# Two expert layers: the last block's results stay on chip and come back by products, row copies wait for the comparisons, parameter loads change queue

## Reference, cut to what matters

```python
x = layer_norm(ALPHA * x + h, ln_g[i, 0], ln_b[i, 0])      # 512 tokens x 1024
# moe_ffn: one of 4 groups of 4 experts for each token, the best 2 of the group
s = sigmoid(x @ w_router); biased = s + b_router
grp = argmax(sum of the two best in each group)
gate = s of the two best experts of grp, divided by their sum
f = sum over experts of ((silu(x @ w_gate) * (x @ w_up)) * gate) @ w_down
x = layer_norm(ALPHA * x + f, ln_g[i, 1], ln_b[i, 1])
```

## Time and profile before

| what | value |
| --- | --- |
| time, median of 3 runs | 2315.68 us (2313.99 to 2317.23) |
| the profiled execution | 2315.13 us, its span in the trace 2313.3 us |
| PE busy in the span | 2025.1 us, 88% |
| DVE busy | 1392.0 us, 60% |
| ACT busy | 946.2 us, 41% |
| POOL busy | 143.0 us, 6% |

### The profile page before, as it was taken

The page is one execution under the profiler, slowest core; times in us unless marked ns, Lnnn a source line. Parts: engine busy times, 40 slices in busy tenths (PEclk is TensorE's granted clock), DMA queues, the critical chain, the costliest instruction groups (busy, mean ns, idle before and its releaser), DMA issues. The chain is left out here.

```text
span 2313.3 us, 29677 instructions
## 1 busy us (share of the span) xinstructions
PE 2025.1 (88%) x11832; PEld 1715.4 (74%) x11832; DVE 1392.0 (60%) x1932; ACT 946.2 (41%) x1387; POOL 143.0 (6%) x196
## 2 busy tenths in 40 slices
PE   5999988979999898999959999299968888599993
PEld 5888878869999785876748888178956666488882
DVE  7864545435545444433379999445036665789995
ACT  4643336221000002534357777221125561477772
POOL 3441000000000000000030000000000000200000
PEclk9999999979999998999969999699879999699996
DMA  7433112232322222220249999422420002189993
GB/s 212 108 74 96 65 55 86 65 63 91 110 73 92 73 76 77 92 74 36 91 143 375 383 397 388 121 77 91 133 57 1 1 1 79 55 344 385 398 390 118
DMA packets 165944, 326.58 MB, mean 141 GB/s; under 512 B 33392, under 2 KB 101792, under 8 KB 165680
## 3 DMA queue, kind: packets, MB, share of 16 engines
q1 hardware_dynamic: 133872, 282.92, 34.6%
q0 software_dynamic: 10720, 30.34, 4.1%
q10 hardware_dynamic: 21216, 11.42, 2.0%
HBM read 299.41 MB, written 19.99 MB: 138 GB/s over the span
## 5 line engine op out<-in xcount | busy, mean ns | idle before, releaser
L2256 PE MATMUL ps<-m_ws,m_xbT 128*128 128x512 f32 x1344 | 314.5, 390 | 0.0
L2256 PEld LDWEIGHTS ps<-m_ws,m_xbT 128*128 128x128 f32 x1344 | 251.8, 188 | 52.1
L2446 DVE TENSOR_TENSOR m_ws<-ring,m_ws 128x2048 fp32r<-128x2048 f32 x112 | 256.1, 2289 | 32.5 <-ACT m_ws L2313 30.0
L1621 PE MATMUL ps<-ffT,ff_ws 128*128 128x264 f32 (+1 forms) x1056 | 241.7, 324 | 4.4 <-DVE ff_ws L431 4.4
L2313 ACT CAST m_ws<-ring 128x2048 fp32r<-128x2048 f32 x112 | 213.3, 1910 | 66.2 <-PE ps L2256 38.4
L1621 PEld LDWEIGHTS ps<-ffT,ff_ws 128*128 128x128 f32 x1056 | 176.8, 190 | 20.2 <-DVE ff_ws L431 4.5
L1621 PE MATMUL ps<-ffT_lo,ff_ws 128*128 128x264 f32 (+1 forms) x528 | 170.3, 323 | 0.0
L2289 PE MATMUL ps<-m_ws,m_hT 128*128 128x512 f32 x672 | 166.8, 397 | 0.0
L2289 PEld LDWEIGHTS ps<-m_ws,m_hT 128*128 128x128 f32 x672 | 122.1, 188 | 23.1
L2443 DVE TENSOR_TENSOR m_ws<-ring,m_ws 128x2048 fp32r<-128x2048 f32 x56 | 128.2, 2290 | 9.5 <-ACT m_ws L2311 8.7
L458 PE MATMUL ps<-fd_ws,fd_xs 128*128 128x512 f32 x528 | 121.9, 394 | 6.7 <-DVE fd_xs L431 6.7
(11 more groups left out here) (521 smaller groups left out, 4260.2 us busy)
## 6 DMA issues: line engine op xcount, KB each, us to landing
ring<-in_moe_w_gate SPq DMA_DIRECT2D x112, 512.0 KB, 5.4
ring<-in_moe_w_up SPq DMA_DIRECT2D x112, 512.0 KB, 7.4
ring<-in_moe_w_down SPq DMA_DIRECT2D x56, 1024.0 KB, 8.0
ring<-in_w_up SPq DMA_DIRECT2D x22, 1024.0 KB, 5.1
ring<-in_w_in SPq DMA_DIRECT2D x16, 1024.0 KB, 6.6
ring<-in_gla_w_in SPq DMA_DIRECT2D x12, 1024.0 KB, 5.3
ring<-in_w_down SPq DMA_DIRECT2D x11, 1024.0 KB, 4.9
ring<-in_nsa_w_in SPq DMA_DIRECT2D x10, 1024.0 KB, 6.7
```

The lines of the kernel that those rows point to most:

```text
L1621: ins = nc.tensor.matmul(ps[:, bank, 0:b - a], w[j][:, k, s * P:(s + 1) * P], x[l][:, k, a:b], start=(k == 0 and j == l), stop=(k == KD - ...
L2256: ins = nc.tensor.matmul(ps[:, it % 2, :], xbT[:, blk % 2, a, 4 * half + k, :].bitcast(F32R), v[b][:, k, :], start=(half == 0 and k == 0 a ...
L2446: ins = V.tensor_tensor(o, x.rearrange("p (j k w) -> p j k w", k=4, j=2), x0, ALU.subtract)
```

## The change

It has four parts. (1) In the head of `moe_stage`, POOL's row copies wait until all one-hots are made; two of the four roundings of ACT, and their rests on DVE, move behind the sigmoid and behind the group choice; `lo(0)` and `lo(1)` move behind the slot numbers; the table for the sigmoid is loaded earlier; blocks 2 and 3 are loaded one unit later. (2) In its tail, block 6 is not copied, stored and fetched: the gather from DRAM takes blocks 0 to 5 (block 6 of `y_slots` is zeroed once) and waits only for these; its sum with `h` comes first; the output of block 6 is split in two halves and 16 products with a transposed one-hot bring its rows to the tokens in PSUM, where `residual` adds them. One-hots of the last block are made in unit 20 and transposed in unit 23. (3) `residual` and `squares` now make LayerNorm's sums in the expert stage, and the norm stage (kind "summed") only makes the reciprocal root and normalises. (4) The parameter loads at the heads of `gla_project` and `nsa_project` are issued by POOL, and DVE waits for them after `lo(1)`.

```diff
 norm_stage:
-            st = self.sb(ctx, tag + "_st", [P, 5, 8])
+            st = self.lst if kind == "summed" else self.sb(ctx, tag + "_st", [P, 5, 8])
...
+                if kind == "summed":
+                    act.wait_ge(self.squared, TT * self.n_ln)
...
-                    for i, (r, t, c0) in enumerate(tiles):
+                    for i, (r, t, c0) in enumerate(tiles if kind != "summed" else ()):
 residual:
-        link(self.nc.vector.scalar_tensor_tensor(y, y, ALPHA, new, ALU.mult, ALU.add, accum_out=st[:, 3, t:t + 1]))
+        link(self.nc.vector.scalar_tensor_tensor(y, y, scale, new, ALU.mult, ALU.add, accum_out=st[:, 3, t:t + 1]))
 gla_project and nsa_project: scalar, vector, gpsimd
-                for to, frm in loads:
-                    act.dma_start(to, frm).then_inc(loaded, 16)
...
-                dve.wait_ge(loaded, 16 * len(loads))
                 S.lo(dve, 0)
                 S.lo(dve, 1)
+                dve.wait_ge(loaded, 16 * len(loads))
...
+                for to, frm in loads:
+                    pool.dma_start(to, frm).then_inc(loaded, 16)
 moe_stage, tensor:
+                        if it == EG * LAST - 1:
+                            pe.wait_ge(hot, 2 * TT)
+                            pe.wait_ge(xt_lo, 2 * (LAST - 2) + 2)
+                            for t in range(TT):
+                                ins = nc.tensor.transpose(ps[:, 7, P * t:P * (t + 1)], hot_flat[:, P * t:P * (t + 1)], self.ident[:])
...
+                pe.wait_ge(yl_out, 2)
+                for t in range(TT):
+                    if t == 3:
+                        pe.wait_ge(centred, 1)
+                    for hf in range(2):
+                        for a in range(2):
+                            ins = nc.tensor.matmul(ps[:, back[t] + hf, :], hot_flat[:, SEQ + P * t:SEQ + P * (t + 1)].bitcast(F32R),
+                                                   (yh, yl)[a][:, 512 * hf:512 * hf + 512].bitcast(F32R), start=(a == 0), stop=(a == 1))
 scalar:
-                        if u in (1, 2):
-                            load_x(u + 1)
+                        if u in (2, 3):
+                            load_x(u)
...
+                act.wait_ge(slab_read, at[units[NU - 1][2]] + 1)
+                for hf in range(2):
+                    nc.scalar.copy(yh[:, 512 * hf:512 * hf + 512].bitcast(F32R), ps[:, 3 + hf, :]).then_inc(yh_out, 1)
+                act.preload_act_table_set("natural_log_exp_and_others")
+                self.squares(act, xb[:, 0, 0:D], centred)
 gpsimd:
+                pool.wait_ge(rl_done, TT)
+                pool.wait_ge(hot, TT)
                 for t in range(TT):
-                    pool.wait_ge(normed, t + 1)
                     nc.gpsimd.tensor_copy(rows[:, t, 0:D].rearrange("p (k q) -> p k q", k=KD),
...
-                for blk in range(NB):
+                for blk in range(LAST):
...
+                for to, frm in ln_loads:
+                    pool.dma_start(to, frm).then_inc(ln_in, 16)
 vector:
+                        if it == EG * (LAST - 1):
+                            link(V.tensor_scalar(slotf[:], slotf[:], -float(P * LAST), None, ALU.add))
+                            for t in range(TT):
+                                V.tensor_scalar(hot_flat[:, P * t:P * (t + 1)].bitcast(F32R), slots[:, 0:P], slotf[:, t:t + 1], None,
+                                                ALU.is_equal).then_inc(hot, 1)
...
+                dve.wait_ge(y_in, 16 * TT)
                 for t in range(TT):
-                    dve.wait_ge(y_in, 16 * TT)
                     V.scalar_tensor_tensor(h[:, t, :], h[:, t, :], ALPHA, rows[:, t, 0:D], ALU.mult, ALU.add).then_inc(h_out, 1)
...
+                for hf in range(2):
+                    dve.wait_ge(yh_out, hf + 1)
+                    V.tensor_tensor(yl[:, 512 * hf:512 * hf + 512].bitcast(F32R), ps[:, 3 + hf, :], yh[:, 512 * hf:512 * hf + 512],
+                                    ALU.subtract).then_inc(yl_out, 1)
+                for t in range(TT):
+                    dve.wait_ge(back_done, t + 1)
+                    self.residual(link, t, ps[:, back[t]:back[t] + 2, :], centred, 1.0)
```

More of the change, by code:

```diff
@@ L2116, in _, with moe_stage @@
                 W.send(sp)
-    def moe_stage(self, tag, units, next_held, xT, yb, first):
+    def moe_stage(self, tag, units, next_held, xT, yb, first, ln_loads):
         nc, ps, W, A, h = self.nc, self.ps, self.W, self.A, self.h
@@ L2160, in moe_stage @@
                 tag, "normed", "turned", "evac", "rs", "rh_done", "rl_done", "hot", "xp_done", "xp_out", "gate_done", "gw_done", "aown")
-            ln_in, squared, lst = self.ln_in, self.squared, self.lst
+            ln_in, squared, lst, n_ln = self.ln_in, self.squared, self.lst, self.n_ln
+            self.n_ln += 1
+            hot_done, hot_out, yh_out, yl_out, back_done, centred = self.sems(
+                tag, "hot_done", "hot_out", "yh_out", "yl_out", "back_done", "centred")
+            LAST = NB - 1
+            assert LAST % 2 == 0
+            hot_flat = onehot[:].rearrange("p t c -> p (t c)")
+            yh, yl = (xbT[:, 1, a].rearrange("p k c -> p (k c)") for a in range(2))
+            back = (0, 5, 3, 0)
+            n_sent = 16 * (TT + (NB + 1 if first else 0))
             (loaded, zeroed, ones_set, rows_in, lg_done, s_out, g_done, cum_done, gid_done, slot_done, sent, xt_done, xt_hi, xt_lo,
@@ L2346, in load_x @@
                     else:
-                        act.wait_ge(sent, 16 * (TT + (NB if first else 0)))
+                        act.wait_ge(sent, n_sent)
                     act.dma_start(xb[:, blk % 2, :], self.x_slots[P * blk:P * (blk + 1), :]).then_inc(x_in[blk % 2], 16)
@@ L2464, in _, with rest_x @@
                 dve.wait_ge(normed, TT)
-                for t in range(TT):
+                def rest_x(t):
                     dve.wait_ge(rh_done, t + 1)
@@ L2604, in second_block, with nsa @@
             self.recycle_semaphores()
-            self.nsa(xT, gb, ln_loads(0, 1), ln_loads(1, 0))
+            self.nsa(xT, gb, ln_loads(1, 0))
             if stop == "nsa":
                 return
-            self.moe_stage("m1", self.n_moe[1], None, xT, gb, False)
-            self.norm_stage("l3", TILES2, h, h, None, "ln", g, b, LN_EPS, loads=ln_loads(1, 1), to_dram=out[0])
-    def nsa(self, xT, gb, loads, next_loads):
+            self.moe_stage("m1", self.n_moe[1], None, xT, gb, False, ln_loads(1, 1))
+            self.norm_stage("l3", TILES2, h, h, None, "summed", g, b, LN_EPS, to_dram=out[0])
+    def nsa(self, xT, gb, next_loads):
         sb = self.sb
@@ L2773, in _ @@
                 S.lo(dve, 10)
+            @block.gpsimd
+            def _(pool):
+                for to, frm in loads:
+                    pool.dma_start(to, frm).then_inc(loaded, 16)
             @block.sync
```

90 lines of the change are left out of this document (57 added, 33 removed).

## The result

The changed kernel took 2285.85 us (median of 4 runs, 2282.59 to 2289.54) against 2316.45 us (4 runs, 2313.99 to 2318.07) for the kernel before beside it: a ratio of 0.9869, 95% interval 0.9851 to 0.9887, so about 30.3 us faster (26 to 35). The profiled execution took 2286.25 us with a span of 2284.4, against 2315.13 and 2313.3.

The account below looks back on a forecast made before the run. PE's products in the middle of the expert stages were taken as the bound, unchanged, with gains only at heads and tails: 4.0 + 4.1 + 2 x 4.2 + 5.6 + 2.6 - 1.0 = 23.7 us, giving 2292 us, range 2281 to 2301.

Parts of the forecast that it names:

- Heads of the projection stages: Starts of gla and nsa: with parameter loads on POOL, DVE's first slab halves start earlier, gaining 4.0 and 4.1 us.
- Head of the expert stage, up to the gather: Expert-stage start: without copies among the normalising, comparisons come 11.3 us and one-hots 9.7 us earlier; ACT is late next.
- Behind the gather: Expert-stage head after the one-hots: four copies block DVE for 7.7 us, so `lo(2)` can start only 4.5 us earlier.
- PE's pause of "over 4 us": Behind unit 0 of the expert stage: PE waits over 4 us for `lo(2)`, so unit 1 runs partly at half rate.
- the 4.2 us per layer: Whole expert-stage head: net gain left in each layer after copies, clock and scatter; bounds 2 and 9.7 us.
- Inside the units: Expert-stage units: DVE's small extra work is hidden, PE's four transposes cost 0.5 us per layer.
- its last rival: Expert-stage units, also called slower: late slabs and colliding scatters make DMA set the pace; 2326 us, chance 0.03.
- Tails: Ends of the expert stages: block 5's earlier store starts the fetch chain sooner, gaining 5.6 us in layer 2, 2.6 in layer 1.
- the forecast's bound: Second layer's tail: the gain falls to 3.5 us if the fetch is 2 us later.
- the copies cost DVE little: Expert-stage heads: row copies slip in where DVE waits or reads PSUM, each head gives 9.7 us; 2281 us, chance 0.14.
- the tails give nearly nothing: Expert-stage tails: the new serial chain is as long as the old, tails give 0 and 2 us; 2301 us, chance 0.17.
- No change: Whole kernel: a later stage absorbs the gains, for example because slabs are not there; 2315 us, chance 0.04.

Follow-up runs that it names:

- experiment 1: Kernel before with only the parameter loads of gla and nsa moved to POOL and DVE's wait for them behind its first two slab halves; 2304.32 us, ratio 0.9949.
- experiment 5: Changed kernel without POOL's four row copies, which a fill with zeros replaces, so the result is incomplete; 2272.32 us, ratio 0.9818.
- experiment 6: Changed kernel with the four row copies on ACT, behind rounding 3 of x, and none on POOL; 2274.74 us, ratio 0.9829.
- experiment 8: Kernel of experiment 6 with its four scatters held back until the gate products of unit 0 are done; 2278.8 us, ratio 0.9843.
- experiment 7: Changed kernel with POOL's row copies behind the gates instead of behind the one-hots; 2287.4 us, ratio 0.9885.
- experiment 3: Changed kernel with expert-stage head and parameter loads put back as before, leaving the tail change alone; 2312.32 us, ratio 0.9989.
- experiment 4: Changed kernel with the tail reordered: products bringing back the kept block come first, additions of the fetched rows last; 2271.6 us, ratio 0.9803.
- the best kernel: Changed kernel with both the row copies on ACT and the products ahead of the additions of the fetched rows; 2262.53 us, ratio 0.9771.

## Why the prediction was right, and where it was off

By the trace the span fell by 28.9 us; the forecast's sum was 23.7. The measured terms are 4.0 and 4.3 for the heads of gla and nsa, 2.7 for the clock in gla, 5.4 and 6.1 for the expert stages up to their last products, 1.5 and 4.4 for the tails: 28.4. So the direction and the places were right, and the range held because heads of the expert stages that gave more (4.1 us together) and a clock term that the forecast lacked (2.7) outweigh tails that gave less (2.3).

**Heads of the projection stages.** Forecast 4.0 and 4.1, measured 4.0 (from the first transpose to the first product 11.29 us before, 7.28 after) and 4.3 (from the start of normalising to the first product 24.78, then 20.48). What the sum lacks is a term for the clock in gla: 2.7 us more, shown by experiment 1: with the shorter pause the granted clock is still 1.00 when the products begin. The forecast had used the pause of 3.16 us with its clock of 0.54 as a guide to what a pause costs; here one of 3.60 us cost nothing. Length of the pause alone does not decide it.

**Head of the expert stage, up to the gather.** The reckoning was right to 2 us: comparisons 13.1 nearer in place of 11.3, one-hots 11.7 in place of 9.7. (The rest of 3.77 us that it calls the first is the second of four in the trace; the sum doesn't hang on it.) The two rests are in the wait for the counts, and ACT is late next, as the forecast put it.

**Behind the gather.** The forecast said that four copies block DVE for 7.7 us; in all they blocked it for 7.2 (8.58 - 1.36). It said that this would fall on slab halves of 4.2 us; it fell on the comparisons instead. The sum on DVE's list is the same, so `lo(2)` came 7.0 us nearer in place of 4.5 mostly because the list had begun 2 us earlier. PE's pause of "over 4 us" was 1.4 us of idle time, since the gate products (1.95) filled the rest, but unit 1 did run partly at half clock. **The term that was mis-sized is the 4.2 us per layer, less the 0.5 inside the units: 3.7 forecast, 5.4 and 6.1 measured.** At the first down product it was 4.2 against 6.5 and 7.7. The size of its mechanism is confirmed: of 11 us gained ahead of unit 0, the copies take 5.4 in each layer (experiments 5 and 6), where the forecast had 5.5 (9.7 - 4.2). What was wrong is the gain that it took them from. How the 5.4 divides: some 1 for late scatters (experiment 8), about 4 for the copies themselves through the late `lo(2)`, which in experiment 6 starts 37.5 us behind the start of normalising (1996.55 - 1959.07) and in the changed kernel 41.5.

The Trainium skill (SBUF — State Buffer, section "SBUF: two separate sides") says that the port pair is locked for a whole instruction and that the other engine blocks fully. The rows bear that out: each copy held one DVE instruction up for 1.6 to 2.0 us, and the first copy waited for slab halves. In a chain in which each instruction waits for the one before, a copy got in at every link until all four were done, so each copy costs DVE nearly its own length once, not in proportion to what DVE works there. Who gets in where DVE has no such wait isn't shown to follow one rule. `lo(0)` and `lo(1)` kept POOL out for both. But in the kernel before a copy that had waited through one rest (1999.50 to 2001.53) went ahead of the next, which was issued at 2001.46 and took 3.74 us, and in experiment 7 the fourth copy went ahead of `lo(2)` behind a cast.

**Inside the units.** 0.5 us was forecast; 1.1 and 1.6 were lost between the first down product and the end of the last, 1.1 of the 1.6 in the wait for `m_hT` named in experiment 8. The transposes of the one-hots don't show: the run with the tail alone took 224.0 and 224.1 us from the first down product to the end of the last, before 223.7 and 224.6. ACT's waits for slabs rose from 4.8 to 27.9 us in layer 2, which the forecast had named as the sign of its last rival; PE waited for `m_ws` once, 1.1 us ahead of unit 1, and never behind it, so the ring, with ACT's and DVE's slack behind it, took them up. The rate was 375 GB/s in place of 364.

**Tails.** Forecast 5.6 in layer 2 and 2.6 in layer 1, measured 4.4 and 1.5. The mechanism is as put: fetch, additions, rests, half-clock products, sums, one behind the other. The size is off by the fetch: it landed 14.9 us behind block 5's store, not 12.5, and 18.3 in layer 1, where 12.5 and 3.7 had been put; the forecast's bound had it 2 us later. Behind PE's last product it landed 6.3 and 9.7 us, not 4 and 7. Why it takes longer than before is open: it does so with the old heads too (experiment 3). Experiment 4 shows that the fetch was what the chain waited for: with the products in its shadow the wait is gone, and the tails give 10.8 us in layer 1 and 10.1 in layer 2 against before (28.55 and 26.87 down to 17.8 and 16.8).

**The rivals.** That the copies cost DVE little fell (experiments 5 and 6). That the tails give nearly nothing fell by the traces (4.4 and 1.5 here, 4.1 and 2.3 in experiment 3, where the rival had 0 and 2), though layer 1 came near it and its sign, a fetch over 8 us behind the last product, is there in layer 1; the total of experiment 3 doesn't tell the two apart. No change and slower fell with the time. Some 1.1 us of the span's difference is chance, in the first block, which the change doesn't touch: gla's first transposes start at 894.48 and before at 895.56; behind its head, nsa gave some 0.5 us back.

## What to carry to other kernels

A block that is fetched through DRAM should be the last thing that the tail waits for: put all work that doesn't need it ahead of the wait, on every engine, and read in the trace whether the wait is still there. GpSimd copies next to DVE were billed here by their number, once each, as soon as they met a chain of dependent DVE instructions; moving them later only moved the bill (experiment 7), and an engine with a wait of the right length in the same stretch (here ACT, 7.4 us for 8.0 us of copies) does them without delaying unit 0 (34.9 us behind the start of normalising with and without). A wait for slabs on ACT says little by itself: 8 and 12 us more of it went with some 1 us of time a layer (experiment 8). Look at PE's waits before blaming the transfers.

## What was not expected of the hardware

- The clock stayed at full speed behind a pause of 3.60 us (all eight traces with the new head of gla), and had fallen behind one of 3.16 in another stage. In the tail of the best kernel the products that bring the block back ran 3.89 us for 16 in layer 2 behind a pause of 2.09 us, in the kernel of experiment 4 5.49 us behind the same pause. What else decides was not tried.
- GpSimd's issue of a scatter took 0.95 to 1.04 us beside an idle DVE and 1.85 to 3.15 us beside DVE's slab halves, which are ordinary subtractions with two inputs in SBUF. In experiment 4, layer 1, a gather stood beside DVE's subtractions of PSUM halves and kept to 0.95 us; beside DVE's additions hardly any stood, so nothing is shown for them. The Trainium skill (SBUF — State Buffer, the same section) tells of such a slow-down for another kind of DVE instruction, its performance mode with two ports.
- One stage, nsa, took from 502.4 to 507.8 us in three kernels with the same code there, and from 496.0 to 501.5 in the eight others, a difference as large as the gain of a tail.
